# Low parts of odd gate slabs on GpSimd instead of VectorE, in the attention stages of a two-block kernel

## The chip, the cores and the metric

One core of one Trainium2 chip. The time is the device time of one execution in microseconds (us). The core has TensorE (PE; its weight loads are PEld), VectorE (DVE), ScalarE (ACT), GpSimd (POOL) and SyncE (SP), which here issues the loads. Each engine runs its own instructions in order; semaphores order them against each other.

## What is computed

Two transformer-like blocks on 256 tokens of width 2048, all in float32. The first has an mLSTM, a bank of state-space groups and an expert layer that gathers rows of two large tables. The second, which matters here, is, cut to its mixing layer:

```python
proj = h @ w_in                               # 2048 -> 8208 + 3 * 2048 gate columns
o_sb  = stick_breaking_attention(rms_norm(q_sb), rms_norm(k_sb), v_sb)       # 6 heads of 128
o_dil = dilated_mixture(rms_norm(q_dil), rms_norm(k_dil), v_dil, slopes)     # 6 heads, 3 dilations
o_gla = rms_norm(gla_chunked(q, k, v, log_a)) * silu(r)                      # 4 heads, gated linear attention
g = sigmoid(gate_cols.reshape(b, t, 3, d))
y = g[:, :, 0] * (o_sb @ w_br_sb) + g[:, :, 1] * (o_dil @ w_br_dil) + g[:, :, 2] * (o_gla @ w_br_gla)
out = y @ w_out                               # then a SwiGLU layer
```

## The kernel before

**Slabs.** Weights stream from HBM through a ring of four slots (`SLOTS = 4`). A slab is 512 rows by 512 columns of a weight matrix, held as 128 partitions by 2048 floats (1 MB). A float32 product is made of three fast ones: each slab is split into a high part, rounded by ScalarE (`high_part`, L344, the copy at L352), and a low part, slab minus high part, by VectorE (`low_part`, L354, the subtraction at L359). TensorE then multiplies left high x slab high, left high x slab low and left low x slab high, for 4 row chunks and 2 token tiles: 24 matmuls of 512 columns a slab. There are two buffers for high parts (`PARTS = 2`), so the high part of slab n can be made only when TensorE is through with slab n - 2.

**Gate slabs.** The gate columns are 12 blocks of 4 slabs, 48 in all. Their products need only h, so the kernel works them in between the steps of the attention: TensorE has small attention products, VectorE and ScalarE the softmax-like work. The low part of a gate slab is written in place, over the slab in the ring (`ring_low`). Each engine has a function that does gate work up to a given slab number, placed by hand between the attention's steps: `gate_loads` (L1869, SyncE, also stores the finished gates), `gate_highs` (L1879, ScalarE; at the second slab of a block also the sigmoid, L1887, of the block before), `gate_lows` (L1897, VectorE) and `gate_slabs` (L1903, TensorE, products at L1920 to L1922; the first slab of a block waits for the sigmoid of the last). An engine that reaches such a call does the gate work there, whatever else it could do; VectorE's low parts thus stand in the queue between attention steps.

**Stages.** Each is a block of the program; all engines meet at its end.
- Stage 1, L1933, slabs 0 to 7 multiplied: head norms of q and k (squares L1966, sums L1967, root by ScalarE L2002, four products L1975) and transposes (L2022) copied out by VectorE and ScalarE.
- Stage 2, L2036, slabs 8 to 13: stick-breaking attention. GpSimd first makes two masks. VectorE: scores out of PSUM, absolute value (L2068), two steps behind ScalarE's exponential and logarithm (L2071, L2072), the low part of slab 10, more steps, sums out of PSUM (L2081), weights (L2086).
- Stage 3, L2152, slabs 14 to 20: dilated attention. GpSimd makes distances (L2161), VectorE the masks (L2178 to L2188), scores (L2191, L2193), maxima, the log-sums (L2201 to L2216) and weights (L2219).
- Stage 4, L2307, slabs 21 to 35: gated linear attention. The log gates (L2351 to L2358), then 8 levels; in level `lv` VectorE makes the exponents of the next level (`exponents`, L2365, lines L2369 and L2371), calls `gate_lows(25 + lv)`, scales q and k with what ScalarE made of the exponents (`scaled`, L2373) and masks and adds the products of this level (L2392 to L2398; L2395 reads PSUM). Then the output norm (L2410 to L2419), whose root waits on ScalarE ahead of the high parts of slabs 34 and 35.
- Behind it, L2517, slabs 36 to 47 and the three branch products follow without attention between them.

Semaphores: ScalarE counts `high_done`, VectorE `low_done`, TensorE `slabs_used`. The wait values come from the slab's number among the split ones (`split_index`), the same for both counters.

Of the kernel before, what the change touches and what calls it, by code (L numbers as in the profile page):

```python
# [29 lines left out]
def build(nc, a, out):  # L30
# [39 lines left out]
    with ctx:  # L70
# [186 lines left out]
        def split_index(g):  # L257

            return g - whole_before[g]

        def slot_free(sp, g):

            old = g - SLOTS
            if old >= 0:
                if is_whole(old) or is_in_place(old):
                    sp.wait_ge(slabs_used, old + 1)
                else:
                    sp.wait_ge(low_done, split_index(old) + 1)

        def issue(sp, sec, n, g):  # L270

# [14 lines left out]
        def stream(sp, sec):  # L286

            s, g0 = SECTIONS[sec], first_slab[sec]
            n = SLOTS
            if s.per == 4 and s.n // 8 > 1:  # L290
                for m in range(SLOTS, 8):
                    issue(sp, sec, m, g0 + m)
                free, off = (slabs_used, 0) if sec == ADA_R else (low_done, g0 - split_index(g0))
                with sp.Fori(1, s.n // 8) as i:
                    for j in range(8):
                        sp.wait_ge(free, i * 8 + (g0 + j - SLOTS + 1 - off))
                        (k0, ks, src), = s.source((i, j // 4) if s.source is ffn_pairs else i * 2 + j // 4, j % 4)
                        slot = (g0 + j) % SLOTS
                        sp.dma_start(ring[:, slot, :, :], src).then_inc(landed[slot], 16)
                n = s.n // 8 * 8  # L300
            for m in range(n, s.n):
                issue(sp, sec, m, g0 + m)
            if sec + 1 < len(SECTIONS):
                for m in range(min(SLOTS, SECTIONS[sec + 1].n)):
                    issue(sp, sec + 1, m, first_slab[sec + 1] + m)
# [8 lines left out]

        def slab(pe, g, outs, lhs, k0, start, stop):

            pe.wait_ge(low_done, split_index(g) + 1)
            last = slab_products(split_index(g) % PARTS, outs, lhs, k0, start, stop)
            last.then_inc(slabs_used, 1)

# [59 lines left out]
        def linear(pe, sec, taken, lhs=left, left_ready=None):  # L380
# [5 lines left out]
            def pair(i, first):  # L386
                for p in range(2):
                    if not first:
                        for t in taken:
                            each = TT // len(taken)  # L390
                            pe.wait_ge(t, i * 2 * each + (p - 1) * each)
                    for j in range(KD // KS):
                        m = p * (KD // KS) + j
                        if first and p == 0 and left_ready:
                            pe.wait_ge(left_ready, KD // KS + j + 1)
                        pe.wait_ge(low_done, i * 8 + (n0 + m + 1))
                        last = slab_products((n0 + m) % PARTS, [(ps[p * TT + t][:, :], t) for t in range(TT)], lhs,
                                             j * KS, j == 0, j == KD // KS - 1)
                        last.then_inc(slabs_used, 1)
# [1464 lines left out]
        staged = spare[:, 3 * TT * NB:4 * TT * NB]  # L1864
        last_gates = view(spare[:, 0:3 * TT * NB], [3, TT, NB])
        s_gate, s_spill = sem("gates_done"), sem("gates_spilled")
        at = {"SP": 0, "PE": 0, "ACT": 0, "DVE": 0}

        def gate_loads(sp, end):  # L1869

# [26 lines left out]
        def gate_lows(dve, end):  # L1897

            for n in range(at["DVE"], end):
                low_part(dve, gate0 + n)  # L1900
            at["DVE"] = end

        def gate_slabs(pe, end):  # L1903

            for n in range(at["PE"], end):
                b, j = divmod(n, 4)
                if j == 0 and b:
                    pe.wait_ge(s_gate, b)
                pe.wait_ge(low_done, split_index(gate0 + n) + 1)
                for k in range(KS):  # L1910
                    for t in range(TT):
                        lh, ll = left(4 * j + k, t)
# [20 lines left out]
        with nc.Block() as block:  # L1933
            @block.sync
            def _(sp):
                gate_loads(sp, 8)

            @block.vector
            def _(dve):
# [96 lines left out]
        with nc.Block() as block:  # L2036
# [5 lines left out]
            def _(g):  # L2042
# [5 lines left out]
                                pattern=[[1, P]], channel_multiplier=-1).then_inc(s_mk, 1)  # L2048
                g.affine_select(out=upto[:, :], in_=upto[:, :], compare_op=ALU.is_gt, fill=0.0, base=0,
                                pattern=[[-1, P]], channel_multiplier=1).then_inc(s_mk, 1)  # L2050

            @block.vector
            def _(dve):
# [98 lines left out]
        with nc.Block() as block:  # L2152
# [5 lines left out]
            def _(g):  # L2158
                di = dist.bitcast(mybir.dt.int32)
                for c, d in enumerate(parts):  # L2160
                    g.iota(di[:, d], pattern=[[-1, d.stop - d.start]], base=c * P, channel_multiplier=1).then_inc(s_di, 1)  # L2161

            @block.vector
            def _(dve):
# [142 lines left out]
        with nc.Block() as block:  # L2307
# [9 lines left out]
            def _(g):  # L2317
# [5 lines left out]
                I32 = mybir.dt.int32  # L2323
                g.iota(apart.bitcast(I32), pattern=[[1, P]], base=0, channel_multiplier=0).then_inc(s_gi, 1)
                g.iota(lmask.bitcast(I32), pattern=[[0, P]], base=0, channel_multiplier=1).then_inc(s_gi, 1)

            @block.vector
            def _(dve):
# [188 lines left out]
        with nc.Block() as block:  # L2517
# [16 lines left out]
            def _(pe):  # L2534
                gate_slabs(pe, B0)
                for nb in range(OB):
                    for j in range(4):
                        g = gate0 + B0 + 4 * nb + j
                        pe.wait_ge(low_done, split_index(g) + 1)
                        for kk in range(KS):  # L2540
                            i, k = br_chunks[KS * j + kk]
                            u = 3 * nb + i
# [134 lines left out]
        with nc.Block() as block:  # L2677
# [5 lines left out]
            def _(pe):  # L2683
# [9 lines left out]
                def pair(i, first, second=False):  # L2693
                    for p in range(2):
                        for j in range(4):
# [3 lines left out]
                            if not first and p == 0 and j == 2:  # L2699
                                if not second:  # L2700
                                    pe.wait_ge(s_fl, i * 1 - 1)
                                transposes(i)
                            pe.wait_ge(low_done, i * 8 + (n0 + m + 1))
                            last = slab_products((n0 + m) % PARTS, [(ps[2 * p + t][:, :], t) for t in range(TT)],
                                                 left, 4 * j, j == 0, j == 3)
                            last.then_inc(slabs_used, 1)
# [95 lines left out]
```

## Time and profile before

| | us |
|---|---|
| Three timed runs | 4000.13, 4005.29 (median), 4006.86 |
| The profiled execution | 3999.28, span 3997.6 |
| Busy in the span | TensorE 2339.1, VectorE 2555.6, ScalarE 796.2, GpSimd 1255.1 |
| 2607 to 2670, stage 1 | TensorE 57.0, VectorE 47.9, GpSimd 0 |
| 2670 to 2731, stage 2 | TensorE 49.3, VectorE 35.5, GpSimd 0.9 |
| 2731 to 2797, stage 3 | TensorE 54.3, VectorE 40.9, GpSimd 0.5 |

An instruction's row gives its start, how long it took, the line, the operation with output and input tiles and their shapes, and in brackets how long the engine had stood idle and who released it. A line can be a helper's: all low parts are L359, all high parts L352. The recorded time of an instruction begins when its engine takes it up, so time in which it is held up inside the engine counts as its own. GpSimd's busy time is nearly all in the expert layer of the first block; in the attention it makes masks only.

### The profile page before, as it was taken

The numbers are of one execution on the slowest core, as the hardware profiler recorded it, in microseconds if no ns is written. First come the engines' busy times: TensorE is split into PE (matmuls) and PEld (weight loads), VectorE is DVE, ScalarE is ACT, GpSimd is POOL, SyncE is SP. The second block draws the span as 40 slices with busy tenths as digits, with TensorE's granted clock in tenths as the row PEclk, the third lists the DMA queues.
The fourth block names the chain that finished last, engine by engine and source line by source line (L and its number), as shares of the span: only waits on it lengthen the run. The fifth ranks groups of instructions, "written<-read, shape, count | busy, mean of one in ns | idle before, by whom it ended". The sixth has DMA issues, their size and how long they took to land. (4 is left out here: it accounts for less than half of the span.)

```text
span 3997.6 us, 28594 instructions
## 1 busy us (share of the span) xinstructions
PE 2339.1 (59%) x10328; PEld 1725.5 (43%) x10328; DVE 2555.6 (64%) x2380; ACT 796.2 (20%) x655; POOL 1255.1 (31%) x705
## 2 busy tenths in 40 slices
PE   6889888930000000000000499988789969999999
PEld 2423456700000000000000388867668758888787
DVE  2545354479999988998888644365855544444444
ACT  1000223300000000000000233234433333333333
POOL 0722000026778888888888200000000000000000
PEclk9889989955555555555555799989999989999999
DMA  7576455499999999999999555433346545555554
GB/s 223 174 282 248 164 211 201 159 401 410 404 383 398 392 376 367 413 416 384 389 380 397 222 192 196 158 116 122 130 169 205 186 147 190 186 190 190 175 196 158
DMA packets 332244, 1029.47 MB, mean 258 GB/s; under 512 B 35256, under 2 KB 35768, under 8 KB 264696
## 3 DMA queue, kind: packets, MB, share of 16 engines
q1 hardware_dynamic: 245896, 490.12, 35.6%
q0 software_dynamic: 73728, 536.90, 33.3%
q10 hardware_dynamic: 12528, 1.19, 0.3%
q8 instruction: 61, 1.00, 0.1%
q14 instruction: 31, 0.25, 0.0%
HBM read 1021.28 MB, written 6.86 MB: 257 GB/s over the span
## 5 line engine op out<-in xcount | busy, mean ns | idle before, releaser
L359 DVE TENSOR_TENSOR slab_low<-ring,slab_high 128x2048 fp32r<-128x2048 f32 x240 | 549.7, 2292 | 711.8 <-ACT slab_high L352 711.8
L352 ACT CAST slab_high<-ring 128x2048 fp32r<-128x2048 f32 x304 | 579.5, 1909 | 1048.1 <-PE bank L338 810.4
L1804 PE MATMUL bank<-ident,nat 128*128 128x128 f32 x32 | 8.9, 433 | 1288.3 <-DVE nat L1660 1288.3
L1615 DVE SCALAR_TENSOR_TENSOR res<-pool,res 128x2048 f32<-128x2048 f32 x256 | 602.9, 2355 | 75.4 <-DMA pool<-in_peer_v,small 43.3
L336 PE MATMUL bank<-slab_high,left_high 128*128 128x512 f32 x1568 | 615.3, 392 | 25.5 <-DVE slab_low L359 25.5
L337 PE MATMUL bank<-slab_low,left_high 128*128 128x512 f32 x1568 | 613.2, 391 | 0.0
L338 PE MATMUL bank<-slab_high,left_low 128*128 128x512 f32 x1568 | 612.9, 391 | 0.0
L1601 DVE CUSTOM_DVE_ANT_0 pool<-pool,nat 128x2048 f32<-128x2048 f32 x256 | 574.3, 2290 | 58.0 <-DMA pool<-in_peer_u,small 48.3
L1754 POOL DMA_INDIRECT pool<-in_peer_v,small x256 | 550.0, 2148 | 102.6 <-issue 68.3
L1804 PEld LDWEIGHTS bank<-ident,nat 128*128 128x128 f32 x32 | 5.7, 217 | 1292.0 <-DVE nat L1660 1292.0
L1754 POOL DMA_INDIRECT pool<-in_peer_u,small x256 | 482.8, 1886 | 160.3 <-DVE small L1601 70.0
L336 PEld LDWEIGHTS bank<-slab_high,left_high 128*128 128x128 f32 x1568 | 296.6, 189 | 87.9 <-DVE slab_low L359 26.6
L338 PEld LDWEIGHTS bank<-slab_high,left_low 128*128 128x128 f32 x1568 | 296.3, 189 | 62.0
L337 PEld LDWEIGHTS bank<-slab_low,left_high 128*128 128x128 f32 x1568 | 296.5, 189 | 61.4
L327 PE MATMUL bank<-ring,left_scratch 128*128 128x512 f32 x640 | 285.7, 605 | 24.2 <-PEq L493 12.9
L359 DVE TENSOR_TENSOR ring_low<-ring,slab_high 128x2048 fp32r<-128x2048 f32 x64 | 146.7, 2292 | 98.8 <-ACT slab_high L352 93.4
L327 PEld LDWEIGHTS bank<-ring,left_scratch 128*128 128x128 f32 x640 | 122.7, 194 | 180.2 <-issue 171.8
L412 PE MATMUL bank<-ring,pool 128*32 128x512 f32 x768 | 137.0, 823 | 95.8 <-DMA ring<-in_w_ada 90.3
L1920 PE MATMUL bank<-slab_high,left_high 128*128 128x512 f32 x384 | 159.8, 416 | 55.9 <-DVE ring_low L359 42.9
L1921 PE MATMUL bank<-ring_low,left_high 128*128 128x512 f32 x384 | 155.8, 406 | 0.0
L1922 PE MATMUL bank<-slab_high,left_low 128*128 128x512 f32 x384 | 155.0, 404 | 0.0
L336 PE MATMUL bank<-slab_high,hidden_high 128*128 128x512 f32 x352 | 138.3, 393 | 7.1 <-DVE slab_low L359 7.1
(508 smaller groups left out, 2592.9 us busy)
## 6 DMA issues: line engine op xcount, KB each, us to landing
ring<-in_w_in SPq DMA_DIRECT2D x148, 1024.0 KB, 4.9
ring<-in_w_ada SPq DMA_DIRECT2D x96, 1024.0 KB, 8.0
ring<-in_w_ffn_in SPq DMA_DIRECT2D x88, 1024.0 KB, 4.8
ring<-in_w_ffn_out SPq DMA_DIRECT2D x44, 1024.0 KB, 5.0
ring<-in_w_out SPq DMA_DIRECT2D x32, 1024.0 KB, 5.1
ring<-in_peer_wq SPq DMA_DIRECT2D x16, 1024.0 KB, 5.6
ring<-in_w_br_gla SPq DMA_DIRECT2D x8, 1024.0 KB, 5.0
gate_rows<-slab_low_scratch SPq DMA_DIRECT2D x9, 512.0 KB, 5.9
```

The lines of the kernel that those rows point to most:

```text
L327: last = nc.tensor.matmul(o, raw_left[:, k0 + k, t * P:(t + 1) * P], ring[:, slot, k, :], start=start and k == 0, stop=stop and k == KS - 1)
L336: nc.tensor.matmul(o, lh, high[:, part, k, :], start=first, stop=False)
L337: nc.tensor.matmul(o, lh, low[:, part, k, :], start=False, stop=False)
L338: last = nc.tensor.matmul(o, ll, high[:, part, k, :], start=False, stop=final)
L352: nc.scalar.copy(high[:, n % PARTS], ring[:, g % SLOTS]).then_inc(high_done, 1)
L359: eng.tensor_tensor(dst, ring[:, g % SLOTS], high[:, n % PARTS].bitcast(F32), ALU.subtract)\
L1601: v.tensor_tensor_reduce(out=rows_[r], in0=rows_[r], in1=nat[:, t, :], scale=1.0, scalar=0.0, op0=ALU.mult, op1=ALU.add, accum_out=dots[:, ...
L1615: v.scalar_tensor_tensor(res[:, t, :], rows_[r], actv[:, t, bass.ds(i * GB + r, 1)], res[:, t, :], ALU.mult, ALU.add).then_inc(s_free, 1)
L1754: g.indirect_dma_start(rows_[r], None, src, bass.IndirectOffsetOnAxis(st[:, r:r + 1], 0))\
L1920: nc.tensor.matmul(o, lh, hi, start=first, stop=False)
L1921: nc.tensor.matmul(o, lh, ring_low[:, g % SLOTS, k, :], start=False, stop=False)
L1922: return nc.tensor.matmul(o, ll, hi, start=False, stop=final)
```

## The change

The low parts of gate slabs 1, 3, 5, ... 35 (`POOL_GATES = 36`, 18 slabs) are subtracted by GpSimd, in a new function `odd_lows` called in stages 1 to 4 behind GpSimd's masks; it counts a semaphore of its own, `s_odd`. `gate_lows` on VectorE skips them, TensorE waits on the one counter or the other, and every wait on `low_done` behind the gates takes the new number `low_index`, smaller by the slabs that VectorE no longer does. The even gate slabs, the odd ones from 37 on and all other slabs stay on VectorE, at their places. Nothing is moved in the other engines' programs.

```diff
+        POOL_GATES = 36
+
+        def on_pool(n):
+
+            return n < POOL_GATES and n % 2 == 1
+
+        def low_index(g):
+
+            return split_index(g) - sum(on_pool(n) for n in range(max(0, g - first_slab[GATES])))
...
                 else:
-                    sp.wait_ge(low_done, split_index(old) + 1)
+                    sp.wait_ge(low_done, low_index(old) + 1)
...
         def gate_lows(dve, end):
 
             for n in range(at["DVE"], end):
-                low_part(dve, gate0 + n)
+                if not on_pool(n):
+                    low_part(dve, gate0 + n)
             at["DVE"] = end
+
+        def odd_lows(g, end):
+
+            for n in range(at["POOL"], end):
+                if on_pool(n):
+                    i = split_index(gate0 + n)
+                    g.wait_ge(high_done, i + 1)
+                    slot = (gate0 + n) % SLOTS
+                    g.tensor_tensor(ring_low[:, slot], ring[:, slot], high[:, i % PARTS].bitcast(F32),
+                                    ALU.subtract).then_inc(s_odd, 1)
+            at["POOL"] = end
 
         def gate_slabs(pe, end):
...
-                pe.wait_ge(low_done, split_index(gate0 + n) + 1)
+                if on_pool(n):
+                    pe.wait_ge(s_odd, n // 2 + 1)
+                else:
+                    pe.wait_ge(low_done, low_index(gate0 + n) + 1)
...
+            @block.gpsimd
+            def _(g):
+                odd_lows(g, 9)
...
+                odd_lows(g, 15)
...
+                odd_lows(g, 22)
...
+                odd_lows(g, 37)
```

## Rows read from the trace of the kernel before

**Rows 1.** Busy us by engine, then granted TensorE clock, DMA share, GB/s.

```profile
2797.00:2942.00 145.00, 112.93 (x542) 93.01 (x542) 115.04 (x111) 54.29 (x44) 0.88 (x4) 0.93 0.36 117
...
2942.00:3020.00 78.00, 72.06 (x314) 58.68 (x315) 32.26 (x18) 29.59 (x23) 0.00 (x0) 1.00 0.67 240
```

**Rows 2.** TensorE's waits, 2607 to 2942: releaser, total us, times, longest.

```profile
PE bank L1920 <- DVE ring_low L359: 42.5, 12, 10.0
```

**Rows 3.** Line L359: shortest/median/longest ns, first and last start.

```profile
L359 DVE TENSOR_TENSOR ring_low<-ring,slab_high x64: 2281/2292/2295, 2609.3 to 3098.2; 128x2048 fp32r<-128x2048 f32 x64
```

**Rows 4.** Order of time, GpSimd near 110 us: start, us, instruction.

```profile
110.38 0.72 POOL L757 TENSOR_TENSOR parts_scratch<-parts_scratch 128x256 f32<-128x256 f32 x1
```

**Rows 5.** Lines L962, L963, L958 (VectorE) and L672 (GpSimd), columns as in rows 3.

```profile
L962 DVE TENSOR_TENSOR pool<-pool,res x8: 1224/1226/2476, 140.8 to 390.2; 128x1024 f32<-128x1024 f32 x8
...
L963 DVE TENSOR_TENSOR pool<-pool,res x8: 1216/1218/3361, 143.2 to 391.3; 128x1024 f32<-128x1024 f32 x8
...
L958 DVE TENSOR_TENSOR pool<-bank,pool x16: 681/681/692, 135.8 to 359.9; 128x512 f32<-128x512 f32 x16
...
L672 POOL TENSOR_TENSOR pool<-pool,parts_scratch x4: 2345/2352/3219, 129.0 to 314.6; 128x1024 f32<-128x1024 f32 x4
```

**Rows 6.** Order of time, VectorE and GpSimd between 140 and 146 us.

```profile
140.22 1.93 POOL L671 TENSOR_TENSOR parts_scratch<-parts_scratch 128x1024 f32<-128x1024 f32 x1
...
140.75 2.48 DVE L962 TENSOR_TENSOR pool<-pool,res 128x1024 f32<-128x1024 f32 x1
...
142.22 3.21 POOL L672 TENSOR_TENSOR parts_scratch<-parts_scratch 128x1024 f32<-128x1024 f32 x1
...
143.15 3.36 DVE L963 TENSOR_TENSOR pool<-pool,res 128x1024 f32<-128x1024 f32 x1
```

**Rows 7.** Order of time, stage 1: VectorE, TensorE, ScalarE.

```profile
2612.84 1.75 DVE L1966 TENSOR_TENSOR slab_low_scratch<-pool 128x1536 f32<-128x1536 f32 x1
...
2624.54 0.50 PE L1920 MATMUL bank<-slab_high,left_high 128*128 128x512 f32 x1
...
2636.18 0.24 ACT L2002 ACTIVATE small<-small 128x48 f32<-128x48 f32 x1 [3.90 <-DVE small L1969]
...
2636.44 1.28 ACT L1894 ACT_TABLE_LOAD   x1
```

**Rows 8.** Order of time, stage 2: ScalarE, VectorE, TensorE.

```profile
2689.50 1.88 ACT L352 CAST slab_high<-ring 128x2048 fp32r<-128x2048 f32 x1
...
2689.63 2.56 DVE L2071 SCALAR_TENSOR_TENSOR pool<-slab_low_scratch,pool 128x2304 f32<-128x2304 f32 x1 [8.86 <-ACT pool L2100]
...
2692.22 1.36 DVE L2072 TENSOR_SCALAR slab_low_scratch<-slab_low_scratch 128x2304 f32<-128x2304 f32 x1
...
2693.62 2.29 DVE L359 TENSOR_TENSOR ring_low<-ring,slab_high 128x2048 fp32r<-128x2048 f32 x1
...
2695.97 0.79 PE L1920 MATMUL bank<-slab_high,left_high 128*128 128x512 f32 x1 [9.37 <-DVE ring_low L359]
```

**Rows 9.** Order of time, stage 3: VectorE and ScalarE.

```profile
2733.88 0.90 DVE L2178 TENSOR_SCALAR pool<-slab_low_scratch 128x384 int32<-128x384 int32 x3 [3.76 <-POOL slab_low_scratch L2161]
...
2751.12 1.90 ACT L352 CAST slab_high<-ring 128x2048 fp32r<-128x2048 f32 x1
...
2751.24 2.29 DVE L359 TENSOR_TENSOR ring_low<-ring,slab_high 128x2048 fp32r<-128x2048 f32 x1
```

**Rows 10.** Order of time, levels of stage 4: ScalarE and VectorE.

```profile
2842.80 2.29 DVE L359 TENSOR_TENSOR ring_low<-ring,slab_high 128x2048 fp32r<-128x2048 f32 x1
...
2853.09 2.29 DVE L359 TENSOR_TENSOR ring_low<-ring,slab_high 128x2048 fp32r<-128x2048 f32 x1
...
2842.80 1.06 ACT L2440 ACTIVATE slab_low_scratch<-slab_low_scratch 128x1024 f32<-128x1024 f32 x1 [0.22 <-DVE slab_low_scratch L2371]
```

**Rows 11.** Order of time, end of stage 4: ScalarE and VectorE.

```profile
2928.46 3.68 ACT L352 CAST slab_high<-ring 128x2048 fp32r<-128x2048 f32 x2
...
2932.88 2.29 DVE L2416 TENSOR_TENSOR pool<-pool,small 128x2048 f32<-128x2048 f32 x1
```

More of the change, by code:

```diff
@@ L292, in stream @@
                     issue(sp, sec, m, g0 + m)
-                free, off = (slabs_used, 0) if sec == ADA_R else (low_done, g0 - split_index(g0))
+                free, off = (slabs_used, 0) if sec == ADA_R else (low_done, g0 - low_index(g0))
                 with sp.Fori(1, s.n // 8) as i:
@@ L315, in slab @@
         def slab(pe, g, outs, lhs, k0, start, stop):
-            pe.wait_ge(low_done, split_index(g) + 1)
+            pe.wait_ge(low_done, low_index(g) + 1)
             last = slab_products(split_index(g) % PARTS, outs, lhs, k0, start, stop)
@@ L395, in pair @@
                             pe.wait_ge(left_ready, KD // KS + j + 1)
-                        pe.wait_ge(low_done, i * 8 + (n0 + m + 1))
+                        pe.wait_ge(low_done, i * 8 + (low_index(g0) + m + 1))
                         last = slab_products((n0 + m) % PARTS, [(ps[p * TT + t][:, :], t) for t in range(TT)], lhs,
@@ L1866, in build @@
         s_gate, s_spill = sem("gates_done"), sem("gates_spilled")
-        at = {"SP": 0, "PE": 0, "ACT": 0, "DVE": 0}
+        s_odd = sem("odd_gate_low_parts")
+        at = {"SP": 0, "PE": 0, "ACT": 0, "DVE": 0, "POOL": 0}
         def gate_loads(sp, end):
@@ L2538, in _ @@
                         g = gate0 + B0 + 4 * nb + j
-                        pe.wait_ge(low_done, split_index(g) + 1)
+                        pe.wait_ge(low_done, low_index(g) + 1)
                         for kk in range(KS):
@@ L2702, in pair @@
                                 transposes(i)
-                            pe.wait_ge(low_done, i * 8 + (n0 + m + 1))
+                            pe.wait_ge(low_done, i * 8 + (low_index(g0) + m + 1))
                             last = slab_products((n0 + m) % PARTS, [(ps[2 * p + t][:, :], t) for t in range(TT)],
```

## The prediction, written before the changed kernel ran

> **What bounds the kernel now.** First the busy times by stretch, to see which part the change touches and which engine is full there. The 48 gate slabs are multiplied between 2607 and 3020 us; the changed ones (slabs 0 to 35) lie in the attention, which ends near 2948. In its last and longest stretch VectorE is busy 115.0 of 145 us and TensorE 112.9, while GpSimd does 0.88; in the stretch behind it TensorE takes 72.1 of 78 us and VectorE is half idle [rows 1]. Next the waits of TensorE: it stood 42.5 us in 12 waits for low parts, the longest 10.0 [rows 2]. Each low part costs VectorE 2.29 us [rows 3]. So the attention is a chain of VectorE steps with low parts queued between them, and 18 of these, 41 us of VectorE, leave. If they left for nothing, the kernel would gain. What decides is what GpSimd's version costs VectorE.
>
> **The price on GpSimd.** No row shows a 128x2048 subtraction there. Of dense additions and subtractions it did 256 columns in 0.72 us and 1024 in 2.35 (median) [rows 4, 5]: 1.63 us for 768 columns, so 2048 take 2.35 + 1024/768 x 1.63 = 4.5 us. The L671 form (a product, inputs spread from smaller tiles) is lighter, 1.93 for 1024 [rows 6]; twice that, 3.8, is the low end. I take 4.5, the nearer kind of operation. The high end, 5.5, allows for rounding to the other output type, which no GpSimd row has.
>
> **What it does to VectorE.** L962 and L963 of VectorE, both inputs in SBUF, take 1.22 us in the median and reach 2.48 and 3.36; L672 of GpSimd takes 2.35 and reaches 3.21 [rows 5]. The order of time says why [rows 6]. L962 was issued at 140.75, while GpSimd's L671 ran to 142.15; it ended at 143.23, that is 1.22 after L671's end with hardly a gap. L672, issued at 142.22, ended at 145.43: 2.35 after VectorE was through reading. L963, issued at 143.15, ended 1.1 after that. The two take turns whole instruction by whole instruction, and whoever asked first goes first. L958, with one input in PSUM, ran beside GpSimd and never took more than 0.692 [rows 5]. So a GpSimd subtraction stops every VectorE instruction with two SBUF inputs for up to 4.5 us, and most of the attention's are such: the trade is 2.2 us saved (2.29 less the overlap of neighbours) against up to 4.5 paid.
>
> Single-input SBUF instructions in VectorE's fast form (L2072: 2304 columns in 1.36 us, where two-input L1966 needs 1.75 for 1536 [rows 7, 8]) are unknown: nothing in the trace sets one against GpSimd. I work both ends and take the middle, since the row that waits and the row that doesn't are equally near.
>
> The Trainium skill has a rule here (SBUF — State Buffer, "Who interferes with whom"): a tensor_scalar or copy in its two-port mode holds the pair shared with GpSimd, as a two-input instruction does. By it the upper end below holds in stages 2 and 3, and the sum would be 31 instead of 28 us. No row here shows it.
>
> **Stage by stage**, times as us after 2600, every step against the order before.
>
> Stage 1 (slabs 0 to 7). High part 1 is ready at 11.1, low 0 holds VectorE's inputs to 11.5, GpSimd runs to 16.0. The squares issued at 12.84 [rows 7] wait 3.2 us; low 1 is gone, so low 2 comes 0.9 late and slab 2 starts at 25.4 instead of 24.54. Subtraction 3 then holds the next squares 2.7 us, against 2.2 saved. ScalarE's root, which waited for VectorE at 36.18 [rows 7], comes 1.5 late, and behind it table load, sigmoid and slab 4: +1.6. Subtraction 5 meets the four products of the head norms: +0.4. Stage: +2.0.
>
> Stage 2 (slabs 8 to 13). TensorE waits 9.37 us for low 10, which stands behind L2071 and L2072 [rows 8]. High 11 is ready at 91.4; GpSimd takes its turn when L2071 is through at 92.1 and runs to 96.6. Low 10 (93.62 before) then waits until 96.6 (+2.9), or, if L2072 waits as well, until 98.0 (+4.4). Slab 10 and all behind it move by that; low 11 and 13 were off the path, so their removal gives nothing. Stage: +3.7.
>
> Stage 3 (slabs 14 to 20). Subtraction 15 starts at 33.9 with the first mask step [rows 9]. At the low end it stops VectorE for 2.0 us, against 2.2 saved by low 15; low 16 gets in ahead of subtraction 17; that one then delays the row maxima by 1.6; and subtraction 19, issued at 68.5 just ahead of the small log-sum steps, holds them to 73.4, so the weights come 3.9 late. At the high end the mask steps wait 4.2 us, low 16 meets high 17 (ready at 53.0 [rows 9]), loses its turn and comes 6.3 late, and the stage loses 8.5. Stage: +6.2, middle of 3.9 and 8.5.
>
> Stage 4 (slabs 21 to 35). Subtraction 23 stops L2354 for 3.2 us; low 23 is gone and TensorE was busy with slab 23 meanwhile: +0.4. Then eight levels, each 10.29 us of VectorE without a gap (low 26 at 242.80, low 27 at 253.09 [rows 10]). An odd level (low 25, 27, 29, 31 gone) saves 2.2, but that low part covered ScalarE's exponential, 1.06 us and a hand-over [rows 10], which is now waited for: 1.1 is left. Its subtraction, issued when high 27 is ready, falls on the exponents of the next level, all of them two-input, and stops them for 4.5: +3.4 an odd level, 13.6 for four. For the case that one or two fall on the PSUM step (1.29 us) or on the exponential I take off 1.6: 12. Subtraction 33 meets idle time. High 35 is ready at 332.1 [rows 11]; GpSimd takes its turn after low 34 and runs from 332.7 to 337.2, and the product of 2.29 us issued at 332.88 [rows 11] waits 4.3. It is on the chain to the transposes and slab 35; low 35's removal gives 0.4 back. +3.9. Stage: 0.4 + 12 + 3.9 = 16.3.
>
> Behind slab 36 nothing changes; the load queue follows the slabs used, as before, and the other queues get no new order. GpSimd's masks come before its subtractions in each stage, so no mask is late. The new waits stand on GpSimd alone and have only subtractions behind them. TensorE's half-speed stretches at the start of late slabs (one slab then takes 7.3 instead of 5.7) may become a few more: in the range.
>
> Sum: 2.0 + 3.7 + 6.2 + 16.3 = 28.2 us. On the profiled execution (span 3997.6, 3999.28 in all) that is 4027.5. The median of the three timed runs is 4005.29, 6 us above it, though one of them was 4000.13; the mean of all four is 4002.9, and 4002.9 + 28.2 = 4031.
>
> **Rivals.**
> Fewer collisions. Turns are taken, but subtractions fall on PSUM steps, reductions and idle time more often than I walked it. With half the price: +8 to +18, about 4016. For: VectorE is idle a fifth of the last stretch. Against: the levels have no gaps.
> Faster (the other side). No stop of VectorE in these stages, only less work: the table load behind the root gets hidden in stage 1 (1.3), low 16 and the maxima come earlier in stage 3 (2.9), four levels save 1.1 each (4.4), and 0.4 at slab 35: 9.0 us, 3994. It decides if VectorE's two-input instructions keep their medians beside GpSimd. The only rows on it speak against [rows 5, 6].
> Gain and price cancel: within 8 us of 4003. It needs both fewer collisions and the shorter 3.8 us.
> Heavier. The subtraction takes 5.5 us or more, or TensorE's clock falls for more of the slabs: 18 x 1 us nearly all on the path, +45, 4048.
>
> **Numbers.** Forecast 0.62 (its own range +18 to +38: 4021 to 4041), fewer collisions 0.17, cancelling 0.08, faster 0.07, heavier 0.06. The range leaves out the faster and cancelling cases and most of the heavier: 4011 to 4044. A measurement tells 0.2%, 8 us, from no change. Slower: 0.62 + 0.17 + 0.06 = 0.85; same: the 0.08 and the near half of the faster case, which lies at that bound, 0.11; faster: 0.04.
>
> **What would show it.** GpSimd would have 18 instructions of 4.5 us at least, some recorded up to 2.5 longer for waiting; VectorE 46 low parts of ring_low instead of 64, and L1966, L2068, L2369, L2371, L2416 with maxima 3 to 4.5 above their medians; TensorE's wait before slab 10 up from 9.4 to 12 or 14 us; two levels together 24 us instead of 20.6; the product behind low 34 ending near 339 plus the shift. It would be wrong if those VectorE maxima stay at their medians, if GpSimd's subtraction is far from 4.5, or if TensorE stands waiting for odd low parts, which I expect nowhere for more than a microsecond.

## The result, and the profile after

| | before | after |
|---|---|---|
| median of 5 runs | 4005.29 (4000.13 to 4008.09) | 4045.72 (4032.66 to 4056.45) |
| profiled execution, span | 3999.28, 3997.6 | 4045.72, 4044.0 |

The changed kernel is slower: ratio 1.010, 95% interval [1.0074, 1.0125]. Forecast was slower, 4031, range 4011 to 4044; measured 40.4 us more instead of 28.2, and 1.7 us outside the range.

The changed kernel's lines are shifted: L359 is now L369, L1966 is L1996, L2072 is L2103, L2178 is L2210, L2369 and L2371 are L2402 and L2404, the scaling steps L2375 and L2376 are L2408 and L2409, L2416 is L2449; GpSimd's subtraction is L1922. Where the time went is read from the order of time of TensorE after the change: the first matmul of stages 1, 2, 3 and 4, and the first of slab 36 behind the attention.

```profile
2615.80 1.08 PE L2052 MATMUL bank<-ident,pool 128*128 128x128 f32 x4 [0.54 <-PEq L1522]
...
2682.01 0.76 PE L2145 MATMUL bank<-nat 128*128 128x256 f32 x1 [3.21 <-PEq L1959]
...
2749.59 0.35 PE L2288 MATMUL bank<-pool 128*128 128x128 f32 x1 [2.30 <-PEq L2066]
...
2824.94 0.27 PE L2488 MATMUL bank<-ident,small 128*16 128x128 f32 x1 [2.30 <-PEq L2183]
...
2998.43 0.47 PE L1946 MATMUL bank<-slab_high,left_high 128*128 128x512 f32 x1 [3.39 <-PEq L2339]
```

The starts differ by 66.2, 67.6, 75.3 and 173.5 us, 382.6 in all. The same marks before (2607.3, 2671.1, 2733.3, 2799.1, 2951.4) give 63.8, 62.2, 65.8 and 152.2, together 344.0. So 38.6 us of the profile's 46.4 arose in the attention; 8.5 came before it, where the programs are the same, and 0.6 went the other way behind it. I call the time between the first and the last mark the stretch. It is compared below, and not the whole profile: the first mark lay anywhere between 2607 and 2628 us in the twelve profiles of this case, with the same program up to it.

Busy time in the stretch, columns as in [rows 1], before:

```profile
2607.30:2951.40 344.10, 279.33 (x1321) 229.71 (x1321) 244.24 (x250) 140.04 (x145) 2.29 (x10) 0.92 0.37 123
```

and after:

```profile
2615.80:2998.40 382.60, 287.84 (x1320) 237.06 (x1321) 253.26 (x232) 140.00 (x145) 89.37 (x28) 0.87 0.33 110
```

VectorE lost 18 of its low parts and is 9.0 us busier. GpSimd went from 2.3 to 89.4 us. TensorE stood idle 94.8 us of the stretch instead of 64.8, and its granted clock fell from 0.92 to 0.87.

The subtraction of GpSimd (instructions, busy us, mean ns, idle us), then VectorE's lines as in [rows 3], after the change:

```profile
L1922 POOL TENSOR_TENSOR ring_low<-ring,slab_high 128x2048 fp32r<-128x2048 f32 x18 | 87.1, 4840 | 629.5 <-ACT slab_high L362 629.5
...
L369 DVE TENSOR_TENSOR ring_low<-ring,slab_high x46: 2279/2292/6474, 2617.8 to 3146.9; 128x2048 fp32r<-128x2048 f32 x46
...
L1996 DVE TENSOR_TENSOR slab_low_scratch<-pool x4: 1752/3008/4790, 2621.3 to 2637.3; 128x1536 f32<-128x1536 f32 x4
...
L2103 DVE TENSOR_SCALAR slab_low_scratch<-slab_low_scratch x1: 5534/5534/5534, 2704.9 to 2704.9; 128x2304 f32<-128x2304 f32 x1
...
L2210 DVE TENSOR_SCALAR pool<-slab_low_scratch x3: 346/348/4654, 2750.1 to 2755.0; 128x384 int32<-128x384 int32 x3
...
L2402 DVE TENSOR_TENSOR slab_low_scratch<-slab_low_scratch x8: 1224/1225/5175, 2850.2 to 2934.5; 128x1024 f32<-128x1024 f32 x8
...
L2404 DVE SCALAR_TENSOR_TENSOR slab_low_scratch<-slab_low_scratch x8: 1224/1225/5399, 2855.4 to 2935.8; 128x1024 f32<-128x1024 f32 x8
...
L2449 DVE TENSOR_TENSOR pool<-pool,small x1: 6407/6407/6407, 2976.5 to 2976.5; 128x2048 f32<-128x2048 f32 x1
```

The reader is to see the third number of the triples, the longest. Every one of these lines has its old duration as the shortest and one instruction or more far above it: 1.75 became 4.79, 1.36 became 5.53, 0.35 became 4.65, 1.22 became 5.40, 2.29 became 6.41 and 6.47. GpSimd's mean is 4.84, the 4.5 worked out in the prediction and what it waited itself. Not every instruction that the prediction named was hit: L2068, now L2099, took the same 2.56 us. Set against experiment e1 below, where GpSimd subtracts nothing, thirteen of VectorE's instructions in the stretch took 2.5 to 4.4 us longer, 49.1 us together, and the others the same within 0.15.

Stage 2 in order of time, the counterpart of [rows 8]:

```profile
2702.29 2.56 DVE L2102 SCALAR_TENSOR_TENSOR pool<-slab_low_scratch,pool 128x2304 f32<-128x2304 f32 x1 [11.27 <-ACT pool L2131]
...
2704.06 5.15 POOL L1922 TENSOR_TENSOR ring_low<-ring,slab_high 128x2048 fp32r<-128x2048 f32 x1 [16.64 <-ACT slab_high L362]
...
2704.89 5.53 DVE L2103 TENSOR_SCALAR slab_low_scratch<-slab_low_scratch 128x2304 f32<-128x2304 f32 x1
...
2710.45 2.29 DVE L369 TENSOR_TENSOR ring_low<-ring,slab_high 128x2048 fp32r<-128x2048 f32 x1
...
2712.80 0.80 PE L1946 MATMUL bank<-slab_high,left_high 128*128 128x512 f32 x1 [14.05 <-DVE ring_low L369]
```

GpSimd asked at 2704.06, while L2102 ran to 2704.85, and then had its 4.4 us; L2103, a single-input instruction in the fast form, was recorded from 2704.89 and ended at 2710.42, that is 1.2 after GpSimd's end at 2709.21. The low part of slab 10 stands behind it, and TensorE waited 14.05 instead of 9.37 us.

### The profile page after: what moved, and what is told of

Its sections match the earlier page's. It is cut to its first block and busy times, and to the rows that moved or that the text cites. A ratio compares the mean times of both kernels' runs of the same rounds, so it can differ in the third digit from the quotient of the medians.

```text
span 4044.0 us, 28587 instructions
## 1 busy us (share of the span) xinstructions
PE 2353.1 (58%) x10328; PEld 1735.5 (43%) x10328; DVE 2565.5 (63%) x2362; ACT 796.1 (20%) x655; POOL 1344.6 (33%) x723
## 5 line engine op out<-in xcount | busy, mean ns | idle before, releaser
L369 DVE TENSOR_TENSOR slab_low<-ring,slab_high 128x2048 fp32r<-128x2048 f32 x240 | 549.7, 2292 | 711.6 <-ACT slab_high L362 711.6
L1611 DVE CUSTOM_DVE_ANT_0 pool<-pool,nat 128x2048 f32<-128x2048 f32 x256 | 575.2, 2290 | 59.7 <-DMA pool<-in_peer_u,small 49.6
L1764 POOL DMA_INDIRECT pool<-in_peer_v,small x256 | 549.5, 2147 | 102.6 <-issue 68.3
L1922 POOL TENSOR_TENSOR ring_low<-ring,slab_high 128x2048 fp32r<-128x2048 f32 x18 | 87.1, 4840 | 629.5 <-ACT slab_high L362 629.5
L369 DVE TENSOR_TENSOR ring_low<-ring,slab_high 128x2048 fp32r<-128x2048 f32 x46 | 113.7, 2471 | 93.1 <-ACT slab_high L362 88.8
```

What stands on the lines that cost most here:

```text
L369: eng.tensor_tensor(dst, ring[:, g % SLOTS], high[:, n % PARTS].bitcast(F32), ALU.subtract)\
L1611: v.tensor_tensor_reduce(out=rows_[r], in0=rows_[r], in1=nat[:, t, :], scale=1.0, scalar=0.0, op0=ALU.mult, op1=ALU.add, accum_out=dots[:, ...
L1764: g.indirect_dma_start(rows_[r], None, src, bass.IndirectOffsetOnAxis(st[:, r:r + 1], 0))\
```

## The experiments

Each was timed beside the kernel before on its chip; the stretch and the stages are read from its own profile as above. TensorE has half-speed pieces: in them a matmul of 512 columns starts every 0.43 us instead of every 0.23, at the lower of its two clock levels. Where they fall moves stages 1 to 3 by up to 3 us each (below), so a difference of less than that in one of these stages says nothing.

| | stages 1, 2, 3, 4 | stretch | ratio to before, interval |
|---|---|---|---|
| before, second profile | 63.5, 62.0, 65.7, 152.2 | 343.4 | |
| changed, second profile | 66.8, 65.9, 75.3, 173.5 | 381.6 | 1.0101 [1.0085, 1.0117] |
| e1 odd low parts left out | 60.5, 65.4, 62.8, 154.4 | 343.1 | 0.9983 [0.9969, 0.9996] |
| e2 fills in their place | 62.4, 64.8, 67.7, 152.7 | 347.5 | 0.9995 [0.9980, 1.0009] |
| e3 stage 4 only | 62.1, 65.3, 68.4, 173.4 | 369.2 | 1.0063 [1.0042, 1.0084] |
| e4 stages 1 to 3 only | 66.6, 65.9, 75.3, 152.4 | 360.1 | 1.0037 [1.0021, 1.0054] |
| e5 exponential first | 64.6, 65.9, 75.4, 172.2 | 378.0 | 1.0089 [1.0072, 1.0106] |
| e6 the same on before | 63.8, 65.3, 68.3, 152.8 | 350.2 | 1.0023 [1.0011, 1.0035] |
| e7 quarters | 63.2, 64.7, 72.8, 165.7 | 366.4 | 1.0057 [1.0040, 1.0074] |
| e8 before, reordered | 63.8, 61.5, 63.9, 144.6 | 333.8 | 0.9973 [0.9961, 0.9985] |

**e1_left_out.** What would it be worth if the subtractions cost nothing?

```diff
-                if on_pool(n):                                # in odd_lows
+                if False and on_pool(n):
...
-                    pe.wait_ge(s_odd, n // 2 + 1)             # in gate_slabs
+                    pe.wait_ge(high_done, split_index(gate0 + n) + 1)
...                                                            # in the product, odd slabs to 35:
-            nc.tensor.matmul(o, lh, ring_low[:, g % SLOTS, k, :], start=False, stop=False)
+            nc.tensor.matmul(o, lh, hi ..., start=False, stop=False)
```

> The changed kernel, with the 18 odd low parts left out altogether: nobody subtracts them, TensorE waits for the high part alone and multiplies it in place of the low part (that part of the computation is left out). The stretch from the first matmul of stage 1 to the first of slab 36 takes 344.0 us before and 382.6 after. Theory (turns at VectorE's inputs cost the time): without any GpSimd subtraction every VectorE instruction is at its median, and the stretch takes 344 - 9 = 335 us, 331 to 339; VectorE still waits 1.1 us for ScalarE's exponential in odd levels. Rival (something else in the change costs, such as the new semaphore or the new order): the stretch stays well above 344.

Timed it is 0.17% below the kernel before, about 7 us of 4010 (2 to 12 by the interval, which holds the 9 expected); the stretch missed: 343.1, not 331 to 339. The engines in the stretch, columns as in [rows 1]:

```profile
2613.00:2956.10 343.10, 282.35 (x1320) 233.83 (x1320) 203.64 (x232) 139.91 (x145) 2.30 (x10) 0.90 0.38 123
```

VectorE is busy 203.6 us against 244.2 before: 40.6 us of work taken off, and 0.9 us of the stretch won. By stages, against the kernel before, it is 3.2 less, 3.1 more, 3.0 less and 2.1 more. The 3.1 in stage 2 are mostly its score products, at half speed (6.9 us for 4.2). In stage 4, where the prediction had reckoned 4.8 us less for this case, the work that left uncovered something else; the rows under e5 show what. So VectorE's load alone is not what bounds the attention. Against the 253.3 of the changed kernel e1 gives the price of the turns: VectorE's instructions were held up for 49.6 us, of at most 18 x 4.5 = 81, and the stretch is 39.5 us longer.

**e2_write_only.** Reads, or the lateness of the odd low parts?

```diff
-                    g.tensor_tensor(ring_low[:, slot], ring[:, slot], high[...].bitcast(F32), ALU.subtract)
+                    g.memset(ring[:, slot], 0.0) ...          # each waits for the one ahead
+                    g.memset(ring[:, slot], 0.0) ...
+                    g.memset(ring[:, slot, 0:2], 0.0) ...
...                                                            # product as in e1; TensorE waits for the last fill
```

> The changed kernel, but GpSimd fills the slab's slot with a constant, two and a half times over one after the other (about 4.5 us, only writes), in place of each subtraction, and TensorE multiplies the high part again in place of the low one (the odd low parts are left out of the computation). TensorE waits for the last fill as it did for the subtraction. Theory (GpSimd's reads hold up VectorE's second input): two-input instructions of VectorE stay at their medians beside the fills, and the stretch takes 335 to 345 us; the fast single-input forms may still be held up. Rival (it is the lateness of the odd low parts, 4.5 us instead of 2.3): the stretch stays near 382.

Stretch 347.5 (a little over the 345), timed no difference from before. VectorE's squares, the exponents, the two fast forms (L2108, L2215) and GpSimd's first fill, columns as above:

```profile
L2001 DVE TENSOR_TENSOR slab_low_scratch<-pool x4: 1747/1754/1759, 2631.6 to 2646.2; 128x1536 f32<-128x1536 f32 x4
...
L2407 DVE TENSOR_TENSOR slab_low_scratch<-slab_low_scratch x8: 1224/1224/1227, 2843.9 to 2913.2; 128x1024 f32<-128x1024 f32 x8
...
L2409 DVE SCALAR_TENSOR_TENSOR slab_low_scratch<-slab_low_scratch x8: 1224/1224/1226, 2845.2 to 2914.4; 128x1024 f32<-128x1024 f32 x8
...
L2108 DVE TENSOR_SCALAR slab_low_scratch<-slab_low_scratch x1: 2167/2167/2167, 2711.3 to 2711.3; 128x2304 f32<-128x2304 f32 x1
...
L2215 DVE TENSOR_SCALAR pool<-slab_low_scratch x3: 1179/1926/2034, 2753.7 to 2757.6; 128x384 int32<-128x384 int32 x3
...
L1923 POOL MEMSET ring<- 128x2048 f32 x18 | 32.5, 1808 | 596.3 <-ACT slab_high L362 596.3
```

GpSimd was nearly as busy as in the changed kernel (85.7 us in the stretch) and TensorE had to wait for its last fill, yet no two-input instruction of the stretch took over 0.05 us longer than in e1. The fast single-input ones did: 1.36 became 2.17, 0.35 up to 2.03. Two-input instructions are held by GpSimd's reads, not its writes; the fast forms by both. With a stretch of 347.5 the lateness of the odd low parts is ruled out as the cause.

**e3_stage4_only and e4_stages123_only.** Do the losses add up?

```diff
-            return n < POOL_GATES and n % 2 == 1
+            return 22 <= n < POOL_GATES and n % 2 == 1        # e3
+            return n < 22 and n % 2 == 1                      # e4
...
-                    pe.wait_ge(s_odd, n // 2 + 1)
+                    pe.wait_ge(s_odd, (n - 23) // 2 + 1)      # e3
```

> GpSimd subtracts only the odd slabs from 23 to 35 (stage 4), VectorE all others. If the stages' losses are independent, as the theory of turns has it, stages 1 to 3 take 191.8 us as before and stage 4 takes 173.5 as in the changed kernel (152.2 before), so the stretch takes 365 us. Rival (one stage's delay carries into the next, through the load queue or TensorE's clock): the parts don't add up to 38.6.

> GpSimd subtracts only the odd slabs from 1 to 21 (stages 1 to 3), VectorE the rest. Theory: stages 1 to 3 take 209.1 us as in the changed kernel (191.8 before), stage 4 152.2 as before, the stretch 361 us. Rival: stage 4 loses too though GpSimd does nothing there.

Stage 4 took 173.4 in e3 and 152.4 in e4, stages 1 to 3 together 207.7 in e4; in ratios 0.63 and 0.37% make up the 1.0%. The losses are independent, within the 3 us that a stage moves by itself. The 369.2 of e3 instead of 365 lies in stages 2 and 3, whose program was that of before.

**e5_exp_first and e6_before_exp_first.** The levels lost more than forecast. VectorE, GpSimd, TensorE and ScalarE in levels of the changed kernel, in order of time:

```profile
2864.05 1.23 DVE L2408 TENSOR_TENSOR pool<-pool,slab_low_scratch 128x1024 f32<-128x1024 f32 x1 [1.23 <-ACT slab_low_scratch L2473]
...
2869.97 5.22 POOL L1922 TENSOR_TENSOR ring_low<-ring,slab_high 128x2048 fp32r<-128x2048 f32 x1 [15.72 <-ACT slab_high L362]
...
2870.87 5.40 DVE L2404 SCALAR_TENSOR_TENSOR slab_low_scratch<-slab_low_scratch 128x1024 f32<-128x1024 f32 x1
...
2876.30 2.29 DVE L369 TENSOR_TENSOR ring_low<-ring,slab_high 128x2048 fp32r<-128x2048 f32 x1
...
2878.65 0.79 PE L1946 MATMUL bank<-slab_high,left_high 128*128 128x512 f32 x1 [8.97 <-DVE ring_low L369]
...
2886.68 1.90 ACT L362 CAST slab_high<-ring 128x2048 fp32r<-128x2048 f32 x1 [9.32 <-PE bank L1948]
...
2888.49 1.06 ACT L2473 ACTIVATE slab_low_scratch<-slab_low_scratch 128x1024 f32<-128x1024 f32 x1
...
2889.67 1.23 DVE L2408 TENSOR_TENSOR pool<-pool,slab_low_scratch 128x1024 f32<-128x1024 f32 x1 [3.12 <-ACT slab_low_scratch L2473]
...
2914.52 1.23 DVE L2408 TENSOR_TENSOR pool<-pool,slab_low_scratch 128x1024 f32<-128x1024 f32 x1 [2.33 <-ACT slab_low_scratch L2473]
...
2940.51 1.23 DVE L2408 TENSOR_TENSOR pool<-pool,slab_low_scratch 128x1024 f32<-128x1024 f32 x1 [3.48 <-ACT slab_low_scratch L2473]
```

L2408 is the scaling that needs ScalarE's exponential. It waited 1.23, 3.12, 2.33 and 3.48 us, 10.2 in all; in the kernel before it waited 0.93 and 0.20 in two levels and nowhere else. Behind the hold-up (5.40, then low 26) TensorE had stood 8.97 us and ran slab 26 in 7.9 instead of 5.8 us; high 28 could start only at 2886.68, and the exponential at 2888.49 stands behind it on ScalarE.

```diff
                 for lv in range(1, LV + 1):                   # ScalarE, stage 4; e5 and e6
-                    gate_highs(act, 25 + lv)
                     act.wait_ge(s_gs, gm[f"diff{lv}"])
                     nc.scalar.activation(ee, ee, ACT.Exp).then_inc(s_gf, 1)
+                    gate_highs(act, 25 + lv)
```

> The changed kernel, but in the eight levels of stage 4 ScalarE makes the exponential of a level ahead of the high part, not behind it. In the changed kernel VectorE waits 1.23, 3.12, 2.33 and 3.48 us for that exponential in levels 1, 3, 5 and 7. Theory (the high part ahead of it is late, since the slab two before ran at half speed after TensorE's wait of 9 us): all four waits fall to about 1.2 us, the bare exponential and hand-over, and stage 4 gets 4 to 6 us shorter (173.5 to about 168.5). Rival (the waits are the exponential itself, or VectorE is held up elsewhere): they stay, and so does the stage.

> The kernel before, with the same reordering on ScalarE as in e5. There VectorE waited for the exponential only 0.93 and 0.20 us in two levels, the low parts hiding the rest. Theory: no change beyond 1.5 us in stage 4 (152.2). Rival (the reordering has a gain of its own): stage 4 shorter by 4 us or more here too.

VectorE in e5:

```profile
2867.74 1.23 DVE L2408 TENSOR_TENSOR pool<-pool,slab_low_scratch 128x1024 f32<-128x1024 f32 x1 [6.43 <-PE bank L2518]
...
2879.17 5.59 DVE L2409 TENSOR_TENSOR pool<-nat,slab_low_scratch 128x1024 f32<-128x1024 f32 x1
...
2891.68 1.22 DVE L2408 TENSOR_TENSOR pool<-pool,slab_low_scratch 128x1024 f32<-128x1024 f32 x1 [1.23 <-ACT slab_low_scratch L2472]
...
2914.52 1.23 DVE L2408 TENSOR_TENSOR pool<-pool,slab_low_scratch 128x1024 f32<-128x1024 f32 x1 [1.22 <-ACT slab_low_scratch L2472]
...
2938.45 1.23 DVE L2408 TENSOR_TENSOR pool<-pool,slab_low_scratch 128x1024 f32<-128x1024 f32 x1 [1.23 <-ACT slab_low_scratch L2472]
```

Three waits fell to 1.22 or 1.23. From the scaling of level 2 to that of level 8 (L2408 to L2408) it took 70.7 us, in the changed kernel 76.5: 5.7 less, of which the waits are 5.3. But the stage gained only 1.3, not 4 to 6, since the first level now waits 6.43 us for TensorE, whose slab comes later by the same order. That the exponential stood behind the high part is shown; the reordering is no remedy. In e6 stage 4 is unchanged (152.8), as the theory has it. e6 was timed 0.23% slower over ten runs; its profile has 5.6 us more in stages 2 and 3, where nothing was changed, but whether the timed runs were slower for the same reason is not shown.

Is the hold-up needed for this? The trace of e1, in which nothing is held up, says no. TensorE at slab 26, and the four waits for the exponential:

```profile
2837.06 1.23 DVE L2409 TENSOR_TENSOR pool<-pool,slab_low_scratch 128x1024 f32<-128x1024 f32 x1 [1.92 <-ACT slab_low_scratch L2474]
...
2847.49 0.80 PE L1946 MATMUL bank<-slab_high,left_high 128*128 128x512 f32 x1 [4.49 <-DVE ring_low L369]
...
2859.00 1.23 DVE L2409 TENSOR_TENSOR pool<-pool,slab_low_scratch 128x1024 f32<-128x1024 f32 x1 [3.61 <-ACT slab_low_scratch L2474]
...
2879.95 1.23 DVE L2409 TENSOR_TENSOR pool<-pool,slab_low_scratch 128x1024 f32<-128x1024 f32 x1 [2.61 <-ACT slab_low_scratch L2474]
...
2900.80 1.23 DVE L2409 TENSOR_TENSOR pool<-pool,slab_low_scratch 128x1024 f32<-128x1024 f32 x1 [2.52 <-ACT slab_low_scratch L2474]
```

They sum to 10.7 us, 10.5 in e2, as against 10.2 with the hold-ups. Slab 26 took 8.4 us in e1, behind a wait of 4.49 us, and 7.9 in the changed kernel, behind one of 8.97. The slabs behind such waits took 7.3 to 8.5 us in e1 and 7.1 to 8.3 in the changed kernel, while in the kernel before five of seven in these levels took 5.7 to 5.8. So slabs went slower and the exponential came late as soon as the odd low parts were gone from VectorE's queue, whoever did them. That is also why e1 won so little in stage 4.

**e7_quarters.** One long hold, or the sum of the holds?

```diff
-                    g.tensor_tensor(ring_low[:, slot], ring[:, slot], ...)
+                    for q in range(KS):
+                        last = g.tensor_tensor(ring_low[:, slot, q], ring[:, slot, q], ...)
+                    last.then_inc(s_odd, 1)
```

> The changed kernel, with each GpSimd subtraction cut into four of 512 columns, one behind the other, about 1.3 us each. Theory (turns are taken by whole instructions): no two-input instruction of VectorE is held up more than about 1.4 us (longest of the 1.22 us steps 2.6 instead of 5.4), they get in between the quarters, but the sum of what VectorE loses stays, 4.5 to 5.2 us a slab, so the stretch stays at 378 to 390 us. Rival (the loss is from the length of one hold, which blocks a low part or a step of the chain for 4.5 us at once): the stretch shortens by 10 us or more.

My expectation failed and its rival fits: 366.4 us, 16 less than unsplit, and 1.0057. The stretch, and the exponents of VectorE with GpSimd's 72 quarters:

```profile
2628.30:2994.70 366.40, 282.52 (x1321) 232.48 (x1321) 237.71 (x232) 140.04 (x145) 129.91 (x82) 0.89 0.36 115
```

```profile
L2406 DVE SCALAR_TENSOR_TENSOR slab_low_scratch<-slab_low_scratch x8: 1224/1226/2184, 2855.8 to 2934.8; 128x1024 f32<-128x1024 f32 x8
...
L1923 POOL TENSOR_TENSOR ring_low<-ring,slab_high 128x512 fp32r<-128x512 f32 x72 | 127.7, 1802 | 581.6 <-ACT slab_high L362 581.6
```

The longest hold of an exponent step is 0.96 us, of any instruction 1.1, inside the 1.4 expected; but the sum did not stay: VectorE is busy 237.7 us, so it was held 34.1 instead of 49.6. GpSimd's subtractions were busy longer, 127.7 us instead of 87.1: more of the waiting was its own. Another 4.1 us of the gain are shorter waits for the exponential (6.1 in all for 10.2). That the rest comes from quarters that fall on steps that don't collide (from PSUM, reductions, waits for another engine) is likely, but was not taken apart.

**before_second and after_second.** How much of a stretch is chance?

> The kernel before once more, unchanged, for a second profile. In e3 and e6 stages 2 and 3, though their program was that of the kernel before, took 65.3 and 68.4 to 68.5 us instead of 62.2 and 65.8: the six score products at their start ran at half of TensorE's speed there. Theory (where the half-speed stretches fall differs between executions of one program): this profile shows 62.2 or 65.3 in stage 2 and 65.8 or 68.5 in stage 3, and stage 4 within 1 us of 152.3. Rival (e3 and e6 differ by their programs): again 62.2 and 65.8.

> The changed kernel once more, unchanged, for a second profile and a ratio on the same chip as the kernel before. Theory: the instructions of VectorE that GpSimd holds up are the same ones by the same lengths (the fast mask step 4.65, the fast L2103 5.53, L2449 6.41), the stretch takes 376 to 385 us, and the timed difference is 30 to 45 us. Rival (the 38.6 us of the first profile were partly chance, as TensorE's half-speed stretches fell): the stretch is 375 or less.

343.4 and 381.6 beside 344.0 and 382.6; the held instructions of the changed kernel that the expectation names are held again by the same length (4.67 for the mask step; in stage 1 one of the squares is held 4.4 us where it was 2.5):

```profile
L2103 DVE TENSOR_SCALAR slab_low_scratch<-slab_low_scratch x1: 5534/5534/5534, 2700.1 to 2700.1; 128x2304 f32<-128x2304 f32 x1
...
L2449 DVE TENSOR_TENSOR pool<-pool,small x1: 6405/6405/6405, 2971.8 to 2971.8; 128x2048 f32<-128x2048 f32 x1
```

So the difference of the stretch is 38 to 39 us, and timed 1.0101. Its rival falls. The first question is not settled. The kernel before showed 62 and 65.7 in stages 2 and 3 twice, e3 and e6 65.3 and 68.3 to 68.4, with the same program there, as the rival has it. But the changed kernel itself did both: its score products took 5.8 us in the first profile (stage 2 67.6) and 4.2 in the second (65.9). One program can show either; what decides it stays open.

**e8_reordered.** If the order bounds the attention, the order should be changed, on the kernel before:

```diff
# stage 2, VectorE
+                gate_lows(dve, 11)                   # low 10, ahead of the wait for the logarithm
                 dve.wait_ge(s_sf, 2)
                 ... L2071, L2072 ...
-                gate_lows(dve, 11)
# end of stage 4: VectorE, ScalarE, TensorE
-                gate_lows(dve, 34)                   # ahead of the products of the last level
+                gate_lows(dve, 35)
-                gate_lows(dve, 35)                   # behind the norm's sums
+                gate_lows(dve, 36)
-                gate_highs(act, 34)                  # ahead of the norm's root
+                gate_highs(act, 36)
-                gate_slabs(pe, 35)                   # ahead of the last transposes
+                gate_slabs(pe, 36)
```

> The kernel before, all low parts on VectorE, with two places changed. In stage 2 the low part of slab 10 stands ahead of VectorE's wait for the logarithm, not behind two steps that follow it. At the end of stage 4 the high and low parts of slabs 34 and 35 stand ahead of the norm's root, and slab 35 is multiplied ahead of the last transposes. It goes by what the traces showed: VectorE idle 8.9 us before L2071 while slab 10's high part lay ready, and TensorE waiting 9.4 and 10.0 us for low parts 10 and 34. If the order of the queues is what bounds the attention, and not VectorE's load, stage 2 gets 5 to 6 us shorter (62.2 to about 56.5) and stage 4 7 to 9 (152.2 to about 144): 12 to 15 us below the kernel before. Rival (VectorE's load bounds it): no gain, since no work is taken off.

VectorE and TensorE in order of time:

```profile
2695.99 2.29 DVE L359 TENSOR_TENSOR ring_low<-ring,slab_high 128x2048 fp32r<-128x2048 f32 x1 [1.99 <-ACT slab_high L352]
...
2702.88 2.56 DVE L2071 SCALAR_TENSOR_TENSOR pool<-slab_low_scratch,pool 128x2304 f32<-128x2304 f32 x1 [4.60 <-ACT pool L2099]
...
2711.34 0.80 PE L2120 MATMUL bank<-pool,upto 128*128 128x128 f32 x2 [6.11 <-DVE pool L2075]
...
2921.72 2.29 DVE L359 TENSOR_TENSOR ring_low<-ring,slab_high 128x2048 fp32r<-128x2048 f32 x1 [3.63 <-ACT slab_high L352]
...
2932.66 2.29 DVE L359 TENSOR_TENSOR ring_low<-ring,slab_high 128x2048 fp32r<-128x2048 f32 x1
...
2935.10 2.29 DVE L2415 TENSOR_TENSOR pool<-pool,small 128x2048 f32<-128x2048 f32 x1
```

Low 10 is done at 2698.3, slabs 8 to 10 run without a gap, and TensorE now waits 6.11 us for the next step of the chain in place of 9.37 for low 10. Low 34 and 35 lie in what was idle time, and L2415 starts 1.2 us after the root, where its counterpart before (L2416) started 7.6 us after it. Stage 4 is 7.6 us shorter, inside 7 to 9; stage 2 only 0.8, not 5 to 6. Its score products ran at half speed in this profile (7.2 us for 4.2); with these 3.0 us given back it would be 3.8, still short. The stretch is 333.8, 10.2 us below the kernel before, 1.9 of them in stage 3, whose program is unchanged. The timed ratio is 0.9973, 11 us (6 to 16 by the interval): faster than both kernels, and its rival, no gain, falls.

## Why the prediction was wrong in size

Right, by its steps: the price on GpSimd (4.5; the undisturbed ones take 4.5 to 4.6). The turns at VectorE's inputs, whole instruction by whole instruction (e2: GpSimd's reads hold two-input steps, its writes don't). That TensorE would wait nowhere over a microsecond for an odd low part (0.4 us, once). That stages don't pass losses on (e3, e4). The mechanism was right; two terms of the sum were mis-sized.

| stage | forecast | measured, two pairs of profiles |
|---|---|---|
| 1 | 2.0 | 2.5 and 3.3 |
| 2 | 3.7 (ends 2.9 and 4.4) | 5.3 and 3.9 |
| 3 | 6.2 (ends 3.9 and 8.5) | 9.5 and 9.7 |
| 4 | 16.3 | 21.3 and 21.3 |

First, "1.1 is left" in an odd level: 2.2 us saved by the low part that leaves, less 1.1 for the exponential that it had covered, 4.4 in four levels. The step saw that the low part had hidden the exponential, but priced it bare. Measured, the four waits are 10.2 us, 1.1 of which the kernel before had already: 9.0 instead of 4.4, 4.6 us more, so that nothing was left of the saving. The exponential stands behind a high part on ScalarE, the high part behind a slab, and the slab ran at half speed. e5 shows the last link: with the exponential ahead of the high part the waits fall to 1.22. e1 shows that it belongs to the leaving of the odd low parts and not to GpSimd: with nothing held up the waits are 10.7. Why these slabs begin at half speed was not tested. The term is nearly the whole miss of stage 4 (5.0): up to the scaling of level 8 the stage grew by 17.0 us where 12.4 were forecast, behind it by 4.3 for 3.9.

Second, "I work both ends and take the middle" for the fast single-input forms: they are held up (5.53 and 4.65), so the upper ends hold, 4.4 and 8.5, and the sum was 3.0 short. This is the rule of the Trainium skill that the prediction quoted (SBUF — State Buffer, "Who interferes with whom"), and the trace agrees.

The 1.6 us taken off for lucky collisions fitted by luck. No subtraction of the four levels fell on a PSUM step, but each held VectorE 4.0 to 4.2 us instead of 4.5: 16.5 in all, where 18 less 1.6 had been reckoned. A small misreading points the same way: L963 and L962 ended 1.08 us after GpSimd, not 1.22 as the prediction has it for L962 (2.48 from 140.75 is 143.23, GpSimd was through at 142.15).

By this account 8.0 us are named (4.6, 0.4 and 3.0) of the 10.4 that the stretch had over the forecast in the first pair of profiles and 10.0 in the second. The other 2.0 to 2.4 lie in stages 1 to 3 and stay open; half-speed pieces move a stage by as much (in the first pair the score products alone took 1.7 longer). In the timed median, 14.7 us over the forecast, there are besides 2.4 from the base, since the forecast started from 4002.9 and the median of the kernel before was 4005.3, and 2 that lie within the interval.

The two halves of the sum tell it in short. The prediction had 9.0 us of gain for the work that leaves and so 37.2 for the hold-ups. e1 and the changed kernel give 0.9 (3.6, were its score products at full speed) and 39.5. The price of GpSimd was about right; the gain to set against it was not there.

Of the rivals, "faster" priced the free case at 9 us. The timed e1, 7 us, doesn't contradict it, but its main term, 1.1 in each of four levels, is the step that failed: stage 4 of e1 took 2.1 us more, not 4.8 less. "Fewer collisions" and the cancelling case didn't occur. "Heavier" had nearly the time, 4048, but not for its first reason: the subtraction takes 4.5, not 5.5. Its second, more slabs at half speed, happened in part: TensorE was busy 287.8 and 282.6 us in the stretch for 279.3 and 277.3 before, and 282.4 in e1, without GpSimd.

## What to carry to other kernels

Before work goes to GpSimd, list what VectorE runs at that time: a two-input instruction from SBUF or a fast single-input one can stand for nearly the whole of a GpSimd instruction that reads SBUF (up to 4.4 of 4.5 us here). If it must go there, cut it short: in quarters the stretch was 16 us shorter than with one piece. Don't count the work taken off as gain before you have left it out and looked: it also covered the latency of another engine, here 9 us of waiting for ScalarE. And a busy engine isn't the bound: taking 41 us of low parts off VectorE was worth 7 timed and 1 in the stretch, while putting three of them (10, 34 and 35, with the high parts and the slab that belong to them) ahead of waits was worth 11 and 10.

## What the runs showed of the hardware that I had not expected

Fast single-input instructions of VectorE are held by GpSimd's writes too (0.35 us became 2.03 beside fills), while two-input ones pass them at 1.22. A cut into quarters lowers the sum of the holds (49.6 to 34.1 us), not only the longest. And TensorE's half-speed pieces fall differently in programs that are the same up to there: the score products of the six heads took 4.2 us in both profiles of the kernel before and 6.9 in e3 and e6, with slab 10 behind them at 7.6 to 7.9 against 8.2, and in the changed kernel 5.8 in one profile and 4.2 in the other; that moves a stage by 3 us either way.
